# Forgetting-attention decode lots of a hybrid decoder step: the order of a lot's pieces on four engines, and the product that closes the values

## What is computed

```
logit[t,s] = q_t.k_s/sqrt(dh) + c_q[t] - c_k[s]     # past: c_k = -(sum of the forgets behind s)
p = softmax(concat(logit over the past, logit over the new tokens))
out = sum over the past of p * v  +  sum over the new tokens of p * v

def wkv_step(S, inp):                                # RWKV-7, one token
    sa = einsum('bhij,bhj->bhi', S, a_t)
    S  = S * w_t + sa * b_t + v_t * k_t
    y  = einsum('bhij,bhj->bhi', S, r_t)
```

## Time and profile before

| | |
|---|---|
| median of 3 runs | 1532.34 us (1529.98 to 1535.18) |
| the profiled execution: its time | 1530.06 us |
| its span | 1528.3 us |
| mean granted clock of TensorE over the span | 0.972 of full speed |
| PE (TensorE matmul) busy | 1425.0 us, 93% |
| DVE (VectorE) busy | 437.5 us, 29% |
| ACT (ScalarE) busy | 358.0 us, 23% |

### The profile page before, as it was taken

How to read it: one execution, slowest core, us unless ns; L and a number is a source line. 1 busy time by engine, 2 the same in 40 slices (tenths; PEclk the granted TensorE clock), 3 DMA queues, 4 the chain that set the end, 5 groups by cost and what they waited for, 6 DMA issues and landing times.

```text
span 1528.3 us, 27895 instructions
## 1 busy us (share of the span) xinstructions
PE 1425.0 (93%) x11595; PEld 965.6 (63%) x11595; DVE 437.5 (29%) x917; ACT 358.0 (23%) x713; POOL 109.8 (7%) x223
## 2 busy tenths in 40 slices
PE   5999999997889899999988789999999999999997
PEld 4755666664567677777755554467777777744442
DVE  5021444445654444444435341210000000000002
ACT  3011222325634344434433432100000000000001
POOL 6292000000000000000301000000000000000000
PEclk9999999998799999999999989999999999999999
DMA  5187011005678788879875989002211131150001
GB/s 203 56 200 195 0 56 35 1 1 179 203 271 271 251 272 274 277 241 307 257 242 185 349 272 329 1 0 76 90 55 55 56 110 55 55 193 0 0 0 62
DMA packets 123174, 219.32 MB, mean 144 GB/s; under 512 B 11451, under 2 KB 35078, under 8 KB 123046
## 3 DMA queue, kind: packets, MB, share of 16 engines
q1 hardware_dynamic: 115154, 193.64, 37.8%
q0 software_dynamic: 7824, 23.85, 5.7%
q10 hardware_dynamic: 68, 0.02, 0.0%
HBM read 203.06 MB, written 14.41 MB: 142 GB/s over the span
## 4 chain that ended last, share of the span: by engine, by line
PE 85%; DVE 5%; DMA 3%; ACT 3%; issue 2%; SPq 1%; POOL 0%; DVEq 0%; POOLq 0%; ACTq 0%
PE PS L1361 22%; PE PS L736 13%; PE PS L1380 10%; PE PS L1170 6%; PE PS L1184 4%; PE PS L1300 4%; PE PS L1229 3%; PE PS L709 2%; DMA arena<-in_cache_k 1%; DMA out_wkv_prompt<-arena 1%; PE PS L814 1%; PE PS L1386 1%; PE PS L984 1%; PE PS L994 1%; PE PS L988 1%
## 5 line engine op out<-in xcount | busy, mean ns | idle before, releaser
L1361 PE MATMUL PS<-arena 128*128 128x288 f32 x1408 | 342.1, 405 | 1.2 <-DVE arena L2241 1.2
L1361 PEld LDWEIGHTS PS<-arena 128*128 128x128 f32 x1408 | 265.8, 189 | 77.3 <-DVE arena L2241 1.4
L736 PE MATMUL PS<-arena 128*128 128x301 f32 (+1 forms) x736 | 197.2, 424 | 0.0
L1614 ACT ACTIVATE arena<-PS 128x512 f32<-128x512 f32 x256 | 141.3, 596 | 192.5 <-PE PS L1170 192.2
L1170 PE MATMUL PS<-arena 128*128 128x128 f32 x1024 | 152.5, 294 | 25.0 <-DMA arena<-in_cache_k 12.6
L736 PEld LDWEIGHTS PS<-arena 128*128 128x128 f32 (+1 forms) x736 | 135.4, 187 | 57.1 <-issue 15.3
L1170 PEld LDWEIGHTS PS<-arena 128*128 128x128 f32 x1024 | 121.2, 150 | 53.8 <-issue 24.3
L1380 PE MATMUL PS<-arena 128*128 128x512 f32 x352 | 151.5, 592 | 1.5 <-DVE arena L2267 1.5
L1380 PEld LDWEIGHTS PS<-arena 128*128 128x128 f32 x352 | 66.5, 189 | 86.2 <-issue 84.2
L2267 DVE TENSOR_TENSOR arena<-PS,arena 128x576 f32<-128x576 f32 x22 | 16.7, 757 | 327.0 <-ACT arena L1678 327.0
L1678 ACT ACTIVATE arena<-PS 128x576 f32<-128x576 f32 x22 | 14.3, 651 | 329.8 <-PE PS L1361 329.8
(11 more groups left out here) (360 smaller groups left out, 1452.5 us busy)
## 6 DMA issues: line engine op xcount, KB each, us to landing
arena<-in_cache_k SPq DMA_DIRECT2D x256, 256.0 KB, 4.2
arena<-in_cache_v SPq DMA_DIRECT2D x256, 256.0 KB, 4.7
arena<-in_w_gate SPq DMA_DIRECT2D x11, 1024.0 KB
arena<-in_w_up SPq DMA_DIRECT2D x11, 1024.0 KB
arena<-in_w_in SPq DMA_DIRECT2D x5, 2048.0 KB, 12.0
forgets_after<-arena POOLq DMA_DIRECT2D x64, 128.0 KB, 8.3
arena<-forgets_after SPq DMA_DIRECT2D x32, 256.0 KB, 4.9
arena<-in_w_down SPq DMA_DIRECT2D x4, 2048.0 KB
```

Of the source, the lines that this page charges most:

```text
L736: ins = mm(PS[0:width, bank, 0:HALF], wring[:, c % 2, k, c0:c0 + width], xnT[:, k, half * HALF:(half + 1) * HALF], start=(k == 0), stop=(k ...
L1361: ins = mm(PS[:, 4 * (f % 2) + 2 * w + half, 0:HO], fring[r % FR][:, c:c + P], hT[:, k, half * HO:(half + 1) * HO], start=(k == 0), stop=( ...
L1614: av(KTs[:, (2 * i + q) % LOT], PS[:, T_USE[("k", L, i, q)] % 2, :].rearrange("p (g n) -> p g n", g=NG), ACT.Copy)\
```

## The change

The diff:

```diff
--- before.py
+++ after.py
@@ -288,20 +288,25 @@
             T_READ.append((reader, n))
 
         for L in range(LOTS + 1):
-            for i in range(LOT + 1):
+            for i in range(LOT):
                 if i == 2 and L:
                     use_t(("p", L - 1), "pr_taken", L)
-                if i < LOT and L < LOTS:
+                if i == 3 and L % NLOT == 0 and L < LOTS:
+                    use_t(("n", L // NLOT), "prn_taken", L // NLOT + 1)
+                if L < LOTS:
                     for q in range(2):
                         use_t(("k", L, i, q), "kt_taken", 2 * LOT * L + 2 * i + q + 1)
-                if L % NLOT == 0:
-                    if i == 2 and L < LOTS:
-                        use_t(("n", L // NLOT), "prn_taken", L // NLOT + 1)
-                    if i == 3 and L:
-                        use_t(("o", L // NLOT - 1), "o_done", L // NLOT)
+            if L % NLOT == 0 and L:
+                use_t(("o", L // NLOT - 1), "o_done", L // NLOT)
+
+        RWKV_DUE = []
+        for piece in range(8 * LOTS):
+            done, aim = RWKV_DUE[-1] if piece else 0, (piece + 1) * N_RWKV / (8 * LOTS - 6)
+            RWKV_DUE.append(min(N_RWKV, done + (done < aim if piece % 2 else done < aim - 1)))
+        assert RWKV_DUE[-1] == N_RWKV
 
         def rwkv_due(piece):
-            return min(N_RWKV, 1 + piece * (N_RWKV - 1) // (8 * LOTS - 20))
+            return RWKV_DUE[piece]
 
         x2 = at(XR0, NTILE, D)
         hT = at(qT_off, KT, OUTC)
@@ -1229,8 +1234,6 @@
                         ins = mm(PS[ROWS[r], OUT, 0:QW], PTs[:, i, ROWS[r]], Vr[:, i, r // 2, QW * (r % 2):QW * (r % 2) + QW],
                                  start=(i == 0), stop=(i == LOT - 1), skip_group_check=True)
                     ins.then_inc(S["v_free"], 1)
-                if half:
-                    mm(PS[:, OUT, 511:512], ident, ones[:, 0:1], start=False, stop=True, skip_group_check=True).then_inc(S["ov_ready"], 1)
 
             def turn_output(pr):
                 pe.wait_ge(S["o_scaled"], pr + 1)
@@ -1244,33 +1247,34 @@
                     pr, j = L // NLOT, L % NLOT
                     turn_keys(L, 0)
                     yield
+                    if L:
+                        page_scores(L - 1, 3)
+                    if j == 0 and L:
+                        new_scores(pr)
+                    yield
                     turn_keys(L, 1)
+                    yield
                     page_scores(L, 0)
                     yield
                     if L:
                         turn_probs(L - 1)
-                    yield
                     turn_keys(L, 2)
+                    yield
                     page_scores(L, 1)
-                    yield
                     if L:
                         lot_values(L - 1, 0)
+                    yield
                     if j == 0:
                         turn_new(pr)
-                    yield
                     turn_keys(L, 3)
+                    yield
                     page_scores(L, 2)
-                    yield
                     if L:
                         lot_values(L - 1, 1)
-                    yield
-                    page_scores(L, 3)
                     if j == 0:
+                        new_values(pr)
                         if L:
                             turn_output(pr - 1)
-                        new_values(pr)
-                    if j == NLOT - 1 and pr + 1 < NPAIR:
-                        new_scores(pr + 1)
                     yield
 
             pe.wait_ge(S["proj_taken"], len(ITEMS))
@@ -1284,6 +1288,8 @@
                     next(rest)
                     done += 1
             assert done == N_RWKV and next(rest, 1) == 1
+
+            page_scores(LOTS - 1, 3)
 
             def rows_of(i):
                 return (slice(64, P), slice(SEQ, OUTC)) if i == 0 else (slice(0, P), slice((i - 1) * P, i * P))
@@ -1628,18 +1634,18 @@
                     pr, j = L // NLOT, L % NLOT
                     take_keys(L, 0)
                     yield
+                    yield
+                    take_keys(L, 1)
                     if L:
                         exp_lot(L - 1)
-                    take_keys(L, 1)
+                    yield
                     yield
                     if L and j == 0:
                         exp_new(pr)
-                    yield
                     take_keys(L, 2)
                     yield
                     yield
                     take_keys(L, 3)
-                    yield
                     yield
                     yield
 
@@ -2126,12 +2132,12 @@
 
             def add_output(L):
                 q = L // NLOT % 2
-                dve.wait_ge(S["ov_ready"], L + L // NLOT + 2)
+                dve.wait_ge(S["v_free"], LOT * (L + 2))
                 dve.wait_ge(S["ov_taken"], L + L // NLOT + 1)
                 stt(Ov[:, q], Ov[:, q], Sb[:, L % 2, 0:1], PS[:, OUT, 0:QW], ALU.mult, ALU.add).then_inc(S["ov_taken"], 1)
 
             def first_output(pr):
-                dve.wait_ge(S["ov_ready"], (NLOT + 1) * pr + 1)
+                dve.wait_ge(S["ov_ready"], pr + 1)
                 v.tensor_copy(Ov[:, pr % 2], PS[:, OUT, 0:QW]).then_inc(S["ov_taken"], 1)
 
             def scale_output(pr):
@@ -2157,6 +2163,12 @@
                     pr, j = L // NLOT, L % NLOT
                     yield
                     if L:
+                        add_scores(L - 1)
+                    if j == 0 and L:
+                        add_new(pr)
+                    yield
+                    yield
+                    if L:
                         add_sums(L - 1)
                     yield
                     if L:
@@ -2166,19 +2178,14 @@
                     if j == 0:
                         take_new_probs(pr)
                     yield
-                    yield
                     if L:
                         add_output(L - 1)
-                    if j == 0 and L:
-                        scale_output(pr - 1)
-                    yield
-                    add_scores(L)
                     if j == 0:
                         if L:
+                            scale_output(pr - 1)
+                        first_output(pr)
+                        if L:
                             take_output(pr - 1)
-                        first_output(pr)
-                    if j == NLOT - 1 and pr + 1 < NPAIR:
-                        add_new(pr + 1)
                     yield
 
             dve.wait_ge(S["rn_taken"], 1)
@@ -2242,6 +2249,7 @@
                 ins.then_inc(S["xnT_ready"], 1)
 
 
+            add_scores(LOTS - 1)
             add_sums(LOTS - 1)
             take_probs(LOTS - 1)
             add_residual(0)
```

More of the change, by code:

```diff
@@ L1251, in all_lots @@
                         turn_probs(L - 1)
+                    turn_keys(L, 2)
                     yield
-                    turn_keys(L, 2)
                     page_scores(L, 1)
-                    yield
                     if L:
                         lot_values(L - 1, 0)
+                    yield
                     if j == 0:
                         turn_new(pr)
+                    turn_keys(L, 3)
                     yield
-                    turn_keys(L, 3)
                     page_scores(L, 2)
-                    yield
                     if L:
                         lot_values(L - 1, 1)
-                    yield
-                    page_scores(L, 3)
                     if j == 0:
+                        new_values(pr)
                         if L:
                             turn_output(pr - 1)
-                        new_values(pr)
-                    if j == NLOT - 1 and pr + 1 < NPAIR:
-                        new_scores(pr + 1)
                     yield
```

## The result

| | median (us) | runs | ratio to before |
|---|---|---|---|
| before, runs beside it | 1533.76 | 4 (1529.98 to 1535.66) | |
| changed kernel | 1549.24 | 4 (1546.26 to 1552.83) | 1.0105, interval 1.0086 to 1.0125 |

The changed kernel is 15.5 us slower (1.05%), where I had forecast 2.7. The two profiled executions differ by more, 1552.83 against 1530.06: that of the changed kernel is the slowest of its four, that of before near the fastest.

The account below looks back on a forecast made before the run. TensorE, busy 514.4 of 576.0 us, was taken to bound the lots stage. Terms -9.9, -3.4, -16.7, +27, +3.5, +3.5 and -1.3 sum to +2.7, forecasting a median of 1535.0 us, range 1519 to 1550.

Parts of the forecast that it names:

- rival 2: Late keys: bias load waits for the later `add_scores`, a lot's keys queue behind it on SP; 1550 us, chance 0.15.
- D: New chain in each lot, late exponential to `take_probs`: TensorE waits for it, +27 us.
- A: Closing product on TensorE, issued 32 times at a pitch of 0.31 us: leaving it out saves 9.9 us.
- B: RWKV steps no longer between TensorE pieces of one shape: saves 3.4 us.
- C: TensorE's old waits for page 0's copies, turned probabilities and keys behind them go: saves 16.7 us.
- E: Three borders of pairs: first scores wait for `add_new` behind the late exponential; +3.5 us, between 0 and 7.
- F: First lots: one more TensorE wait for VectorE's long operations, like the old 3.8; +3.5 us.
- G: Last lots: steps cover old waits, but VectorE's last long RWKV operations move there; -1.3 us, between -7 and +4.
- rival 1: Hidden chain: long steps cover the new chain, leaving only 0.35 in each lot; 1519 us, chance 0.25.
- rival 3: The closing product is nearly free, leaving it out saves only 1.6 us; 1543 us, chance 0.05.
- rival 4: The 15 steps still behind whole-block pieces each bring a wait, some 4 us; 1539 us, chance 0.05.

Follow-up runs that it names:

- run 3: Changed kernel with ScalarE's exponential of a lot again ahead of the copies of page 1's keys; 1536.18 us.
- run 7: Changed kernel plus 16 unread whole-block transposes behind page 0's turn of lot 1; 1541.28 us.
- run 4: Changed kernel with the RWKV steps at the pace of before, still preferring odd pieces; 1559.73 us.
- run 2: Changed kernel with the turn and copy of a pair's new probabilities one piece earlier, ahead of the RWKV step; 1544.24 us.
- run 8: Changed kernel plus 32 unread quarter-column products over 128 rows behind page 0's turn of lot 1; 1542.92 us.
- run 9: Changed kernel plus 16 unread products over 32 rows behind page 0's turn of lot 1; 1558.09 us.
- run 6: Changed kernel with the edits of run 2 and run 3, and lot 2's keys loaded ahead of lot 1's bias; 1527.11 us.
- run 5: Kernel of run 3 with the probabilities' turn and copy also ahead of the RWKV step behind piece 3; 1529.74 us.
- run 11: Changed kernel with the edits of run 2, run 3, run 5 and run 6 together; 1518.13 us, ratio 0.991 to before.
- run 12: Kernel of run 11 plus 16 unread whole-block transposes behind page 0's turn of lot 1; 1516.99 us.
- run 1: Kernel before with only each lot's closing product left out; 1523.89 us, ratio 0.9943.

## Why the prediction was right and wrong

The time lay inside the range, on the side that I held likelier, but more than five times as far out as the forecast; it fell next to the price of rival 2, by another mechanism. That it lies inside is luck: what set the upper end did not happen, and the terms missed both ways, D in lots 4 to 23 by 9 too much, the first lots by 14 too little.

- **A** (-9.9) held: -8.7 measured alone.
- **B and C** can't be told apart, and their sizes are not shown: the middle is 5.8 shorter, but 8.5 us of steps' matmuls left it. The waits for page 0's copies are gone. "Moved at no cost: `add_scores` itself, `new_scores` and the tables" overlooked that the later pace moves four steps from the middle, at full clock, into the last lots, where the mean clock is 0.85.
- **D** (+27) was too large and its cause half wrong. Over the whole span its waits sum to 24.5, within the 20 to 30 that I named, but 5.3 of that is lot 1 and another operation. For lots 4 to 23 I had 23; waits for `take_probs` and for the exponential there sum to 13.9 (14.8 with lot 3). The five lots with L1990's step have 6.1, where I had 6; the five with L984 and L988 have 1.7, where I had 3; the ten with L994 have 6.1, where I had 14. The step that failed is "VectorE then does the work of the step behind piece 3, for which it was waiting: 0.69, with 0.29 until the next operation starts, then `take_probs` 0.69". The changed kernel shows it without the 0.29 and with a wait of the probabilities themselves instead. Timelines of PE, then of DVE, in one lot:

```profile
592.92 0.66 PE L1215 MATMUL PS<-arena 128*128 128x128 f32 x4 [0.29 <-ACT arena L1626]
593.41 0.60 PE L1175 MATMUL PS<-arena 128*128 128x128 f32 x4
594.63 0.66 PE L1175 MATMUL PS<-arena 128*128 128x128 f32 x4 [0.62 <-DVE arena L2127]
```
```profile
593.17 0.68 DVE L1977 TENSOR_TENSOR arena<-PS,arena 128x512 f32<-128x512 f32 x1
593.88 0.69 DVE L2127 COPY arena<-PS 128x512 f32<-128x512 f32 x1
```

  0.91 is lost here where I had 1.4; five of the ten lots look like this, three lose 0.5 and two nothing. And run 3 shows that an earlier exponential leaves the waits for `take_probs` where they were: the wait of keys directly behind probabilities and the step's own operation set them, about half each.
- **E** (+3.5): the three waits are 2.3 each, as worked out; run 3 gave back 3.0 of 6.9.
- **F** (+3.5, bounds 0 to 7) is the step that failed: "No row gives the new wait. It is bounded by nothing and by twice the old; I take one more like it". The first lots took 17.7 more. I looked for one wait, of L883, which did grow (3.8 to 6.2). I did not follow `turn_new`, moved by one piece, past the step behind piece 5, although the reciprocal of 4.15 us stood in the trace. And I priced waits by their own length, when the clock behind them cost more: up to 13.9 of the 17.7 by the upper bound, and some 10, since run 7's first stretch is 9.8 shorter in spite of its added work. I also left out that the new pace makes lot 2's keys late (run 4). The two-fold pitches in the rows of the last lots had shown me such a price, and I used it only there.
- **G** (-1.3): +9.6. The stretch holds four steps more: their matmuls take 55.0 us there, 41.1 before. And its longest wait is for a reciprocal again, on another step; behind it the groups take twice as long until 933 us:

```profile
917.05 2.50 PE L851 MATMUL PS<-arena 32*128 32x320 f32 x4 [4.30 <-DVE arena L2073]
```

  Before, this wait was 3.44, and L846 behind it took 1.34. With the late exponential the stretch took 154 to 156 us in the changed kernel and in runs 2, 4, 7, 8 and 9; I had priced the late exponential in the middle alone. With the early one it took 146.2 and 148.0 in runs 3 and 6, but 153 to 157 in runs 5, 11 and 12, where the probabilities too go ahead of the step; why is left open.
- **Rival 2**: SP's wait for `add_scores` did rise, from 17.1 to 56.9, but waits for keys did not (12.6 before, 10.9 now). Lot 2's keys were late by the step that releases lot 1's bias (SP waited 32.2 for it, before 24.7), not by `add_scores`.
- **Rivals 1, 3 and 4**: 1 would leave 0.35 in each lot, but ten of lots 4 to 23 lose 0.9 or more. 3 fell with run 1. What the 15 steps behind whole-block pieces cost was not tried by itself.

The Trainium skill (TensorE: Matmul & The Clock Gate, section What's actually happening) puts it that "the default state is throttled, and activity releases the throttle." The runs agree that it is work that brings the clock back (385 us with the added transposes, 404 without); they also show 20 us of a busy TensorE at the lower level.

## What to carry to other kernels

Follow each moved instruction past every step on every engine's list, the seldom ones too: one copy of 0.29 us, moved behind one VectorE operation of 4.15, made TensorE wait 3.5, and moving it back gave 5.0. Price a stall of TensorE with the clock behind it, read from the trace as pitches against the same group elsewhere, and look at what work follows the stall. When a steady stretch gets better and the total worse, cut the span into stretches, and compare the work in them (counts of matmuls) and their granted clocks before looking at any single wait: here the shorter middle had only handed four steps on.

## What was not expected of the hardware

Sixteen transposes that nobody reads, 3.4 us of added work, made the kernel 8 us faster, since the granted clock went from 0.50 to 1.00 behind them. For some 20 us of the changed kernel, 384 to 404, TensorE was busy without a gap at the lower level; behind products over 32 rows it stayed there, behind products over 128 rows, whole-block or quarter-column, it rose.
